# A hybrid GLA and sliding-window encoder block: later sums, splits and norm, and the low parts of the token operands made on VectorE alone

## What is computed

```python
h = rmsnorm(x, g_pre)
proj = einsum('btd,de->bte', h, w_in)             # q_a k_a v_a lr z_a q_b k_b v_b z_b m_a m_b
o_a = rmsnorm(gla(q_a, k_a, v_a, decay), g_gla) * silu(z_a)        # called ga below
o_b = sliding_window(rope(q_b), rope(k_b), v_b, sinks) * silu(z_b) # called gb below
y_a = o_a @ w_branch_gla
y_b = o_b @ w_branch_swa
y = sigmoid(m_a + b) * y_a + sigmoid(m_b + b2) * y_b
out = x + rmsnorm(y @ w_out, g_post)
```

## Time and profile before

| | |
|---|---|
| median of 3 runs | 2000.07 us (1998.47 to 2007.79) |
| the profiled execution, its own time | 1996.81 us |
| its span, first to last instruction | 1994.9 us |
| PE busy | 1909.8 us, 96% of the span |
| PE weight loads | 1524.8 us, 76% |
| DVE busy | 1439.0 us, 72% |
| POOL busy | 1056.2 us, 53% |
| ACT busy | 880.1 us, 44% |
| DMA queue of SP | 414.20 MB, 63.2% of 16 engines |
| mean granted TensorE clock | 0.986 |

### The profile page before, as it was taken

How to read it: one execution, slowest core, us unless ns; L and a number is a source line. 1 busy time by engine, 2 the same in 40 slices (tenths; PEclk the granted TensorE clock), 3 DMA queues, 4 the chain that set the end, 5 groups by cost and what they waited for, 6 DMA issues and landing times. The chain is left out here.

```text
span 1994.9 us, 29306 instructions
## 1 busy us (share of the span) xinstructions
PE 1909.8 (96%) x9876; PEld 1524.8 (76%) x9876; DVE 1439.0 (72%) x2219; ACT 880.1 (44%) x1929; POOL 1056.2 (53%) x671
## 2 busy tenths in 40 slices
PE   8999999999999998899999999999999988999896
PEld 7778877777777776777878777777777767777785
DVE  6768876976767667788488887856676676886363
ACT  5457465443444442334267345443444442335421
POOL 5634464644433356668444455553433475768744
PEclk9999999999999998999999999999999999999998
DMA  7524375666776688976433557644767598885862
GB/s 270 167 68 141 116 236 168 217 214 209 227 240 215 198 290 271 349 252 219 146 101 102 166 168 236 216 148 152 224 201 253 182 327 275 311 283 164 309 228 85
DMA packets 280246, 416.06 MB, mean 209 GB/s; under 512 B 33507, under 2 KB 159011, under 8 KB 265635
## 3 DMA queue, kind: packets, MB, share of 16 engines
q1 hardware_dynamic: 280099, 414.20, 63.2%
HBM read 272.10 MB, written 142.02 MB: 208 GB/s over the span
## 5 line engine op out<-in xcount | busy, mean ns | idle before, releaser
L938 PE MATMUL pu<-a_hi,w_hi 128*128 128x512 f32 x1964 | 779.9, 399 | 39.0 <-DVE ct L1839 16.4
L938 PE MATMUL pu<-a_hi,w_lo 128*128 128x512 f32 x1964 | 764.6, 391 | 0.4 <-POOL w_lo L1954 0.4
L938 PE MATMUL pu<-a_lo,w_hi 128*128 128x512 f32 x1964 | 764.0, 391 | 0.0
L1954 POOL TENSOR_TENSOR w_lo<-t,w_hi 128x512 fp32r<-128x512 f32 x276 | 396.5, 1445 | 439.7 <-ACT w_hi L1278 439.4
L1954 POOL TENSOR_TENSOR w_lo<-w_raw,w_hi 128x512 fp32r<-128x512 f32 x259 | 385.1, 1497 | 292.6 <-ACT w_hi L1278 292.5
L938 PEld LDWEIGHTS pu<-a_hi,w_hi 128*128 128x128 f32 x1964 | 370.3, 189 | 137.1 <-issue 57.1
L938 PEld LDWEIGHTS pu<-a_hi,w_lo 128*128 128x128 f32 x1964 | 370.4, 189 | 80.4 <-POOL w_lo L1954 0.8
L938 PEld LDWEIGHTS pu<-a_lo,w_hi 128*128 128x128 f32 x1964 | 370.9, 189 | 72.7
L1278 ACT ACTIVATE w_hi<-t 128x512 fp32r<-128x512 f32 x276 | 170.5, 630 | 208.9 <-DVE t L497 147.5
L1963 POOL TENSOR_TENSOR a_lo<-fill_in,a_hi 128x1024 fp32r<-128x1024 f32 x52 | 141.3, 2718 | 107.3 <-ACT a_hi L1297 107.3
L1278 ACT ACTIVATE w_hi<-w_raw 128x512 fp32r<-128x512 f32 x259 | 158.1, 630 | 21.8 <-PE pu L938 16.7
(11 more groups left out here) (186 smaller groups left out, 2465.9 us busy)
## 6 DMA issues: line engine op xcount, KB each, us to landing
w_raw<-in_w SPq DMA_DIRECT2D x81, 1024.0 KB, 7.0
va_d<-ct SPq DMA_DIRECT2D x32, 256.0 KB
qb_d<-ct SPq DMA_DIRECT2D x32, 256.0 KB
zb_d<-ct SPq DMA_DIRECT2D x32, 256.0 KB
q_s<-qb_d SPq DMA_DIRECT2D x32, 256.0 KB, 3.8
z_s<-zb_d SPq DMA_DIRECT2D x32, 256.0 KB, 3.1
gb_d<-gb SPq DMA_DIRECT2D x32, 256.0 KB, 3.6
za_d<-ct SPq DMA_DIRECT2D x32, 256.0 KB
```

What stands on the lines that cost most here:

```text
L938: return nc.tensor.matmul(dst, weights, moving, start=start, stop=stop, skip_group_check=True)
L1954: TT(flat(w_lo[o.n % NWB][:, :, :]), src, as_f32(flat(w_hi[o.n % NWB][:, :, :])), ALU.subtract) \
```

## The change

Four edits. (1) The splits of the token operands move one slot later, those of A21 and A22 by two, S3 by one and S4 by two, and the loads of A21 to S4 by one or two slots. (2) The sum jobs: those of gb come 8 slots apart in place of 10, the first two of ga move from the yB phase to the end of the projections (slots 184 and 191, where they were at 210 and 216), the last two stand at 218 and 226 (were 222 and 228); so also in `sb` 1. (3) In the plain group of yA the gated product goes back into `gate_a`, without the wait for `ct`; the wait and the addition of `yb` into `ct` follow one slot later, and so do the stores and the next gate loads on SP. The norm moves later: sums at END_AT + 6, spread at + 11, tiles from + 13. (4) Behind the eight operands of the head DVE makes both halves of each low part; POOL makes none.

```diff
@@ -139,9 +139,9 @@
-    for _name, _load, _split, _free in (("A11", -10, -6, -7), ("A12", -9, -5, -6), ("A21", -5, -2, -5),
-                                        ("A22", -4, -1, -4), ("S2", -1, 2, -3), ("S1", 0, 3, -2), ("S3", 3, 7, 6),
-                                        ("S4", 4, 9, -1)):
+    for _name, _load, _split, _free in (("A11", -10, -5, -7), ("A12", -9, -4, -6), ("A21", -4, 0, -5),
+                                        ("A22", -3, 1, -4), ("S2", 0, 4, -3), ("S1", 1, 5, -2), ("S3", 5, 8, 6),
+                                        ("S4", 6, 11, -1)):
@@ -166,22 +166,26 @@
-SUMS = 3
-RB_END = 6
-NORM = {9 + x: x for x in range(16)}
+SUMS = 6
+RB_END = 11
+NORM = {13 + x: x for x in range(16)}
...
-    _jobs = [("gb", BASE[0] + 152 + 10 * j, 0) for j in range(KH)]
-    if _sb:
-        _jobs = [("y", BASE[1] + 82 + 10 * j, 0) for j in range(KH)] + [("gb", BASE[1] + 150 + 10 * j, 0)
-                                                                        for j in range(KH)]
-    _jobs += [("ga", YBASE[_sb] + 4 + 6 * j, 1) for j in range(KH)]
+    _jobs = [("y", BASE[1] + 82 + 10 * j, 0) for j in range(KH)] if _sb else []
+    _jobs += [("gb", BASE[_sb] - 2 * _sb + 152 + 8 * j, 0) for j in range(KH)]
+    _jobs += [("ga", BASE[_sb] - 2 * _sb + 184 + 7 * j, 0) for j in range(2)]
+    _jobs += [("ga", YBASE[_sb] + 12 + 8 * j, 1) for j in range(2)]
...
@@ -565,7 +569,7 @@
-                        sp.wait_ge(gs_out, 16 * 4 * jobs_done(f.sb, "gb"))
+                        sp.wait_ge(gs_out, 16 * 4 * stage_jobs(f.sb))
...
@@ -705,14 +709,14 @@
+                if job.what == "ga":
+                    sp.wait_ge(ga_out, 16 * (16 * job.sb + 8 * (job.j // 2 + 1)))
...
@@ -786,7 +790,10 @@
-                    if g and g.n and not g.fast and g.n in STORED:
+                    if g and g.n and not g.fast and g.n in STORED and g.kind != "yA":
+                        store_tile(g, n)
+                for g, n in ((step(s, lag), n) for n, lag in ((0, 3), (1, 5), (2, 7), (3, 9))):
+                    if g and g.kind == "yA" and not g.fast:
                         store_tile(g, n)
@@ -851,7 +858,7 @@
-                    if e == YA_AT + 2 * n + 2:
+                    if e == YA_AT + 2 * n + 3:
                         load_gate_a(sb, 1, n)
@@ -1551,6 +1558,11 @@
                 TT(flat(lo[:, 0:2, :]), flat(src[:, 0:2, :]), as_f32(flat(hi[:, 0:2, :])), ALU.subtract) \
                     .then_inc(a_lo_d_ok, 1)
+                if f.n >= NHEAD:
+                    dve.wait_ge(a_hi_ok, 2 * f.n + 2)
+                    dve.wait_ge(a_lo_p_ok, f.n)
+                    TT(flat(lo[:, 2:4, :]), flat(src[:, 2:4, :]), as_f32(flat(hi[:, 2:4, :])), ALU.subtract) \
+                        .then_inc(a_lo_p_ok, 1)
@@ -1858,10 +1870,13 @@
                         dve.wait_ge(gate_a_in[c], 32 * (4 * g.sb + 1))
+                        STT(gate_a[c][:, :], gate_a[c][:, :], 1.0, bank[:, :], ALU.add, ALU.mult).then_inc(ya_ok, 1)
+                for c in range(4):
+                    g = step(s, 2 * c + 2)
+                    if g and g.kind == "yA" and not g.fast:
+                        dve.wait_ge(ya_ok, 4 * g.sb + c + 1)
                         ct_free(dve, g, c)
-                        STT(ct[c][:, :], gate_a[c][:, :], 1.0, bank[:, :], ALU.add, ALU.mult).then_inc(ya_ok, 1)
-                        dve.wait_ge(ya_ok, 4 * g.sb + c + 1)
-                        TT(ct[c][:, :], ct[c][:, :], yb[c][:, :], ALU.add).then_inc(y_ok, 1)
+                        TT(ct[c][:, :], gate_a[c][:, :], yb[c][:, :], ALU.add).then_inc(y_ok, 1)
@@ -1979,7 +1994,7 @@
-                if s in SPLIT_AT:
+                if s in SPLIT_AT and SPLIT_AT[s].n < NHEAD:
                     split_fill(SPLIT_AT[s])
```

8 lines of the change are left out of this document (4 added, 4 removed).

## The result

| | before | after |
|---|---|---|
| median | 2002.53 us (4 runs, 1998.47 to 2007.79) | 1967.85 us (4 runs, 1964.39 to 1970.29) |
| profiled execution | 1996.81 us | 1969.14 us |
| its span | 1994.9 us | 1967.2 us |
| DVE busy | 1439.0 us | 1419.2 us |
| POOL busy | 1056.2 us | 919.6 us |

The ratio of the two is 0.9835, 95% interval 0.9808 to 0.9861. The change makes the kernel 33 us faster, with 28 to 38 in the interval. The forecast was 44.5 us faster, 1955 us. In the page's 40 slices the granted clock of TensorE reads 8 in two slices before, not in three, and in one after.

What follows compares the result with a forecast made beforehand. PE, busy 96% of the span, bounds the kernel, and its waits are what can go: 34.7 us in six phases plus 9.8 at the norm, 44.5 off 1996.8, plus 3.3 to the median, gives 1955 us; range 1938 to 1980.

Steps and rivals of the forecast that it cites:

- The norm: Slots 555 to 561: with sums three slots later, PE's wait for POOL's last addition goes; 9.8 us gained of 13.4.
- DVE alone: 52 halves move from POOL to DVE; up to 2.2 us of waiting goes with each, so DVE's load falls or stays.
- Rival (a): DVE becomes the bound in yA and the start of the projections: 9.4 us more than forecast, 1965; chance 0.13.
- The sum jobs: yB stretches: stalls at L1857 and slot 219 go, nothing stays of 14.1 and 14.6 us; moved jobs cost nothing.
- the S3 place: Slot 217 and its likes, where PE wants `u2`: S3 late, costing 0.2 to 5.9 us, taken as 3 per gb phase.
- the six phases: The phases that bring eight operands (yB, yA, projections start, out): 24 us stay of 58.7, 34.7 us gained.
- The gated tiles: yA: PE's 5.0 us wait at slot 241 and its half clock go; 5.5 us stay per phase of ga.
- The splits: S3's load goes out about 740.8, lands 8.1 to 11.5 us later; `u2` 0.2 to 1.3 us late from S3's halves.
- rival (c): Slower: A21's halves delay S2's load, S2 delays S3's; with 11.5 us transfers 87 us stay, 2018; chance 0.03.
- The starts of the projections and out: Slots 264 to 274 and 526 to 554: 3.5 us stay in each, between 1 and 6.3.
- three signs of a wrong forecast: Largest waits for late fills, DVE over 95% busy in a yA stretch, or slots 184 to 205 getting longer.
- The sum: Whole kernel: 34.7 + 9.8 = 44.5 us gained, median 1955 us.

## Why the prediction was right and where it was off

The direction and the places were right, 33 us came in place of 44.5, and the median lies within the range.

- **The norm.** Forecast 9.8 us, found 9.7 in the profile and 8.4 alone. POOL's halves were no part of the condition.
- **DVE alone.** The forecast said that DVE's load falls or stays because the waiting of the earlier trace rows goes, and gave it no term of its own. It was right (1439.0 to 1439.5 us with 52 more operations) and too modest: the edit is worth 14 us alone, the largest of the five single runs, and 19 in the change. Rival (a) is out. DVE's busy time in the yA stretches fell to 77.2 and 75.9 us where the rival had 96.7 and 94.0.
- **The sum jobs, the term that was furthest off.** "The third stands at 218, behind the two `ct3` additions instead of between them, and its buffers have been free for long", and nothing of the old stalls stays. I asked who was in front of the job and not who was behind it. Gate tile 0 stands in DVE's slot 219 behind its last pair, and PE wants that bank at slot 221. The forecast's 3 us per phase of gb was for the S3 place alone, which measured 2.4 and 2.5. The third job added 5.2 in each: 15.6 us in place of 6, and 9.6 of the 11.1 that the six phases missed. The jobs in the projections did cost: "I cost them at nothing" was about 3 us short, not on DVE but in SP's queue, where loads of gb's jobs and of ga's first stand in front of `d_g`. The slots from 184 to 205, which the prediction had watched, did not get longer (77.2 us, 77.4 before).
- **The gated tiles.** The two phases of ga hold 10.0 us where 11 were forecast, a hit. But the reason is not shown: the edit alone gave nothing, because a `t` sum beside POOL's half was late in the same place, and the jobs alone already took the two phases from 19.8 to 13.0. With (1), (2) and (3) and without (4) they hold 15.7. Whether (3) gives anything once (4) is in stays open, since no kernel has everything but (3).
- **The splits.** S3's load went out 17.1 us after R(206) where the forecast had 740.8, or 15.9 after the R(206) of before, because A21's halves, two slots later, hold S2's load and S2's halves hold S3's. By the diff S2's and S1's splits move by two slots as well, not by one as the text on the change says. The transfer took 9.4 us, between the 8.1 and the 11.5 used. This is rival (c)'s chain at its ordinary length: a few us per phase. The starts of the projections and out: 9.5 us in place of 7, of which out has 8.2. What the forecast lacked is the question whether the old slots would be better once the rest is changed: it priced (1) and (4) together. In the package (1) costs 12 us and (4) gives 19.
- **The signs.** None of the three signs of a wrong forecast is there: DVE is busy 84% and 82% of the yA stretches, the slots from 184 to 205 are no longer, and the transfers in the two chains read above took 7.2 to 9.4 us. The stretches of yB were to last about 74 us and last 78.4 and 78.7, and those of yA 91.6 and 92.4 where 93 was said.
- **The sum.** Six phases 35.1 against 24 (11.1 short), slots 275 to 459 3.9, the norm 0.1; in the profiled pair (27.7 us found) the 3.0 us of slots 24 to 199 come on top, which are no effect of the change, and slots 200 to 205 and 460 to 467 gave 1.0 each. That the change without (1) brings 45 us, what was forecast with it, is chance. The single runs do not add up to the change: 8.4, 14.0, 10.2, -0.6 and -18.4 us make 14, and the change gives 33. The rest is interplay, of which the runs price only what (1) and (4) do inside the package.

What stays open: what (2) and (3) are worth inside the package, whether the last two jobs have a place without any stall, between gate tile 0 at slot 219 and the fills of the next phase, and whether the 1.7 us in out are more than spread.

## What to carry to other kernels

Price a moved job by who stands behind it in each in-order queue it enters, its transfers' queue too, and not only by who stands in front. Where two engines block each other, add the waiting inside their busy times before calling one of them full: here 52 operations more cost DVE nothing. And take a package of edits apart in both directions, each edit alone and the package without it: here one edit cost 18 us alone and 12 in the package, and the single runs together explain less than half of what the package gives. Look at a kernel whose edit can't touch a stretch before reading a few us there: here one such stretch differed by 7 us.

## What was not expected of the hardware

Two operations on SBUF operands, on DVE and POOL at once, stretch each other far beyond their own length: a half of 1.22 us took 2.31, a `t` sum of 0.68 took 1.78 to 2.88, a pair of `gx` sums 3.42, and on POOL a weight part of 1.29 took 2.25. In the earlier trace rows DVE's operation ends 0.55 us behind POOL's half, and not with it. Taken over the run, moving 141 us of POOL's work (52 halves) to DVE left DVE's busy time unchanged. And an idle PE is paid for again in unequal parts: after the 2.22 us before slot 217 that slot took 2.81 us, after the 3.27 before slot 221 3.98, and after the 5.25 before slot 537 5.25, near twice the usual 2.72; the granted clock of that stretch is 0.96.
